# Products over the 16 meta tokens: reading 128 rows, 112 of them zero, in place of 16

## The reference

```python
u = rmsnorm(h, norm_g)                       # h: 16 meta tokens, then 512 tokens
hq, hf, hi, hz, aq, ak, av, az, ga, gb = split(u @ w_in)
# branch A, per head: gated linear recurrence, S_t = diag(f_t) S_{t-1} + k_t^T v_t, o_t = S_t^T q_t
f = lb + (1 - lb) * sigmoid(hf);  k = 1 - f;  v = hi
yA = (rmsnorm(oA, hg_norm_g) * silu(hz)) @ w_branch_a
# branch B, per head: differential attention in blocks of 128 queries, causal, meta keys always visible
p = softmax(q1 k1^T * scale) - lam * softmax(q2 k2^T * scale)
yB = (rmsnorm(p @ v, da_norm_g) * (1 - lam_init) * silu(az)) @ w_branch_b
m = sigmoid(ga) * yA + sigmoid(gb) * yB
out = rmsnorm(h + m @ w_out, final_g)[16:]   # the meta tokens are dropped
```

## Time and profile before

| | |
|---|---|
| median of 3 runs | 784.7 us (783.88 to 784.8) |
| profiled execution, span of the core | 782.7 us |
| mean granted TensorE clock | 0.995 of full speed |
| TensorE busy (matmul) | 762.8 us, 97% |
| TensorE weight load busy | 665.0 us, 85% |
| VectorE, ScalarE, GpSimd busy | 60%, 36%, 3% |
| DMA queue of the weights | 26.5% of 16 engines |

### The profile page before, as it was taken

The page is one execution under the profiler, slowest core; times in us unless marked ns, Lnnn a source line. Parts: engine busy times, 40 slices in busy tenths (PEclk is TensorE's granted clock), DMA queues, the critical chain, the costliest instruction groups (busy, mean ns, idle before and its releaser), DMA issues.

```text
span 782.7 us, 13096 instructions
## 1 busy us (share of the span) xinstructions
PE 762.8 (97%) x4689; PEld 665.0 (85%) x4689; DVE 468.4 (60%) x1085; ACT 282.2 (36%) x564; POOL 22.4 (3%) x30
## 2 busy tenths in 40 slices
PE   3999999999999999999999999999999999999996
PEld 2998899889889888988988998898888888888885
DVE  4667668658766865866785686587644333333342
ACT  5414432541452254144234415415532222222132
POOL 1000000000000000000000000000000000000001
PEclk9999999999999999999999999999999999999999
DMA  7411220230122023023112202301232332333602
GB/s 241 134 56 54 82 80 1 79 107 27 54 80 80 27 80 106 1 68 93 54 54 80 80 0 80 107 28 55 81 108 83 105 108 81 106 91 97 238 31 108
DMA packets 105416, 63.18 MB, mean 81 GB/s; under 512 B 2066, under 2 KB 100900, under 8 KB 105396
## 3 DMA queue, kind: packets, MB, share of 16 engines
q1 hardware_dynamic: 105076, 62.26, 26.5%
q10 hardware_dynamic: 320, 0.66, 0.3%
HBM read 60.81 MB, written 2.10 MB: 80 GB/s over the span
## 4 chain that ended last, share of the span: by engine, by line
PE 96%; SPq 1%; issue 1%; DMA 1%; DVE 0%; ACT 0%; POOLq 0%; POOL 0%; DVEq 0%; ACTq 0%
PE ps L361 26%; PE ps L362 25%; PE ps L363 25%; PE ps L469 3%; PE ps L544 3%; PE ps L573 2%; PE ps L574 2%; PE ps L453 1%; PE ps L564 1%; PE ps L551 1%; PE ps L510 1%; PE ps L509 1%; PE ps L476 1%; PE ps L516 1%; PE ps L492 1%
## 5 line engine op out<-in xcount | busy, mean ns | idle before, releaser
L361 PE MATMUL ps<-uT_hi,w_hi 128*128 128x264 f32 (+2 forms) x904 | 315.2, 349 | 0.0
L362 PE MATMUL ps<-uT_lo,w_hi 128*128 128x264 f32 (+2 forms) x904 | 299.0, 331 | 0.0
L363 PE MATMUL ps<-uT_hi,w_lo 128*128 128x264 f32 (+2 forms) x904 | 298.9, 331 | 0.0
L361 PEld LDWEIGHTS ps<-uT_hi,w_hi 128*128 128x128 f32 x904 | 171.2, 189 | 17.1
L363 PEld LDWEIGHTS ps<-uT_hi,w_lo 128*128 128x128 f32 x904 | 170.7, 189 | 16.2
L252 DVE TENSOR_TENSOR w_lo<-w_raw,w_hi 128x1024 fp32r<-128x1024 f32 x104 | 126.3, 1221 | 96.4 <-ACT w_hi L247 95.3
L362 PEld LDWEIGHTS ps<-uT_lo,w_hi 128*128 128x128 f32 x904 | 171.5, 190 | 12.5
L247 ACT ACTIVATE w_hi<-w_raw 128x1024 fp32r<-128x1024 f32 x104 | 110.0, 1057 | 87.8 <-PE ps L363 84.3
L778 ACT ACTIVATE e<-ps,small 128x144 f32<-128x144 f32 (+2 forms) x48 | 22.9, 483 | 71.5 <-DVE small L1179 71.5
L1125 DVE TENSOR_REDUCE small<-sq 128x4 f32<-128x512 f32 x16 | 11.0, 686 | 47.8 <-ACT sq L767 47.8
L1075 DVE TENSOR_TENSOR kk<-kk,tt 128x264 f32<-128x264 f32 (+1 forms) x48 | 20.6, 429 | 25.0 <-PE ps L469 20.7
(11 more groups left out here) (184 smaller groups left out, 1070.2 us busy)
## 6 DMA issues: line engine op xcount, KB each, us to landing
w_raw<-in_w_in SPq DMA_DIRECT2D x80, 512.0 KB, 3.7
w_raw<-in_w_branch_a SPq DMA_DIRECT2D x8, 512.0 KB, 3.6
w_raw<-in_w_branch_b SPq DMA_DIRECT2D x8, 512.0 KB, 3.6
w_raw<-in_w_out SPq DMA_DIRECT2D x8, 512.0 KB, 3.7
x_in<-in_x SPq DMA_DIRECT2D x4, 512.0 KB, 7.9
x_res<-in_x SPq DMA_DIRECT2D x4, 512.0 KB, 6.5
out<-y_out SPq DMA_DIRECT2D x8, 256.0 KB, 2.2
rope<-in_c_rope SPq DMA_DIRECT2D x1, 528.0 KB, 5.9
```

Source lines behind the costliest of these rows:

```text
L361: pe.matmul(dst, w[0], rhs[0], start=start, stop=False, skip_group_check=True)
L362: pe.matmul(dst, w[0], rhs[1], start=False, stop=False, skip_group_check=True)
L363: return pe.matmul(dst, w[1], rhs[0], start=False, stop=stop, skip_group_check=True)
```

## The change

Four fills ahead of the head loop set the meta tile of `pT`, `v_b`, `v_a` and `k_tok` to zero in all 128 rows. In the loop ScalarE and VectorE write rows 0 to 15 as before, and the two products read 128 rows. The fills add to `g_pre`, for which ScalarE waits ahead of the first head's sections, and VectorE in its preparation of the decay constants.

```diff
@@ block.gpsimd
             pool.memset(half_neg, -0.5).then_inc(g_pre, 1)
+            for tail in (pT[:, CH, :], v_b[:, CH, :], v_a[:, CH, :], k_tok[:, CH - 1, :]):
+                pool.memset(tail, 0.0).then_inc(g_pre, 1)
             pool.wait_ge(g_pre, 1)
@@ state_sums
-                pe.matmul(g[:, 0:P], k_tok[0:META, CH - 1, :], v_a[0:META, CH, :], start=True, stop=True) \
+                pe.matmul(g[:, 0:P], k_tok[:, CH - 1, :], v_a[:, CH, :], start=True, stop=True) \
                     .then_inc(hg_done, 1)
@@ attend
-                pe.matmul(dst, pT[0:META, CH, :], v_b[0:META, CH, :], start=False, stop=True) \
+                pe.matmul(dst, pT[:, CH, :], v_b[:, CH, :], start=False, stop=True) \
                     .then_inc(at_done, 1)
@@ block.scalar
+            act.wait_ge(g_pre, 5)
             for n in range(AHEAD):
@@ block.vector
+            dve.wait_ge(g_pre, 5)
             dve.wait_ge(a_pre, 3)
```

## The result

The changed kernel takes 770.02 us (median of 4 runs, 769.36 to 770.25) against 784.75 us (the kernel before, the three runs of above and one more): a ratio of 0.9817, 95% interval 0.9805 to 0.9829, which is 14.7 us off. The forecast was 770.6 us and 14.1 us off. The profiled execution has a span of 768.4 us, where the forecast said 768.6.

The account below looks back on a forecast made before the run. TensorE was taken as the bound, never waiting long in the head loop. Attention 12.5 us plus state sum 1.6 us made 14.1 us off: span 768.6 us, plus 2.0 us to the median, 770.6 us; full range 769.0 to 774.2.

Parts of the forecast that it names:

- The fills are hidden: Four GpSimd fills ahead of its first power: some 0.3 us each, 1.2 us in sum, wholly under 5.3 us idle.
- Rival 3: Fills at GpSimd's arithmetic rate, 77 us in all, hold up the start by 72 us: 842 us; chance 2%.
- The narrowest handover: VectorE's probabilities of block 2 to TensorE's transposes: 0.25 us of room left after the change, 0.06 us needed.
- rival 1: TensorE reaches block 2's transposes early and waits, giving back up to 0.40 us a head: 773.8 us; chance 12%.
- The weight slots have room of microseconds: Weight handovers to TensorE in the head loop: claimed microseconds of room, so no wait when TensorE gets there earlier.
- the two terms: Savings in the head loop: 12.5 us from 32 attention products and 1.6 us from 8 state-sum products.

Follow-up runs that it names:

- e1: Changed kernel with the state sum put back to 16 rows, so only the attention product reads 128 rows: 771.84 us, ratio 0.9838 to the kernel before.
- e6: Changed kernel with block 0's scores also reading 128 rows, using two zero-padded query copies per head on ScalarE: 770.46 us, ratio 0.9828 to the kernel before.
- e9: Changed kernel with only VectorE's copy for the low part of the next weight section moved ahead of level 6: 770.40 us, ratio 0.9820 to the kernel before.

## Why the prediction was right

- **TensorE is the bound and waits for nothing in the heads.** Right: its list of waits has the same three rows from the start of the kernel, and the saved time comes out of the head period one for one.
- **A change of height costs some 0.19 us, and the height itself nothing.** Right, and shown from four sides: the two parts alone (0.39 and 0.20 us a product), 96 rows (no cost), 64 rows (one change between sum and scores gone, none in attention), and another order in the sum (no change). For attention this is 4 x 8 x 0.39 = 12.5 us from the periods of e1, as forecast; for the state sum 1.6, as forecast. Blocks 0 and 1 both gave 0.39, where the prediction had 0.38 and 0.40. Its guess that the new weights are loaded with nothing beside them fits the rows of the loads; what goes on inside the engine no run shows. The Trainium skill's "TensorEngine Tiling (Array Packing)", section "Key Properties", says that changing the mode drains the engine. These runs agree in so far as each change of height costs 0.19 us and 96 rows beside 128 cost nothing; they don't show a drain as such. The Trainium skill's sentence that one matmul with K=32 takes as long as one with K=128 ("TensorE: Matmul & The Clock Gate", "Why this matters for your kernels") doesn't carry over to a short product in a stream of full ones: that product costs 0.39 us on top. No run here times one by itself.
- **The fills are hidden.** Right. GpSimd's timeline of the changed kernel:

```profile
0.78 0.20 POOL L343 MEMSET pT<- 128x128 f32 x1
...
1.20 0.20 POOL L343 MEMSET k_tok<- 128x128 f32 x1
6.10 0.55 POOL L349 TENSOR_TENSOR small<-small 128x1 f32<-128x1 f32 x1 [4.70 <-DVE small L956]
```

  0.20 us each (0.3 was estimated), all over by 1.4 us; the first power starts at 6.10 us. Rival 3 is out by 4.7 us of idle time.
- **The narrowest handover holds.** Right where it looked, 0.26 us of room for 0.25 forecast, and rival 1 did not come. The survey was incomplete, though. "The weight slots have room of microseconds" is wrong for the section behind level 7, whose low part is ready 0.05 us before its load, in the kernel before too (135.50 and 135.55 us). It cost the forecast nothing only because none of the saved changes lies between level 6, from which VectorE's chain starts, and this section. In e6 one did, and its saving was lost there.
- **The size.** 14.1 us forecast, 13.9 from the period, 14.7 by the medians. Each of the two terms is right where it is measured alone; with both in, a head saves 0.03 us less than their sum, 0.2 us in eight heads, and no run isolates why. What the 14.7 has above 13.9 is not in the heads of these traces; the stretch ahead of the first one and the spread of the runs are left for it. The changed kernel measured again is 784.25 - 770.49 = 13.8 us under the kernel before beside it.

## What to carry to other kernels

On a TensorE that never waits, count the places where the row height of neighbouring products changes, not the rows (16, 64, and 96 or 128 together, were three heights here). A lone short product between full ones got cheaper when its operands were filled up with zeros, once, ahead of the loop. For short products that already stand in pairs of one height it brought 0.05 us of 0.66 and took two copies a head (e6). Read the cost from the starts of neighbouring passes: the share of busy time says nothing (97% before and after), since the gap is inside what counts as busy. Before taking time out of one place, look for the next handover behind it that has no room, for each operand that TensorE waits for, the weights too.

## What the runs showed of the hardware

- Products of 64 rows, one on rows 0 to 63 and one on rows 64 to 127, start in pairs, 3 to 9 ns apart. They win back most of what their changes of height cost: two changes and two pairs took 0.66 us, four full-height passes 0.61 us, both with the section pass ahead.
- The stretch ahead of the first head differs from run to run by more than 1 us with the same instructions on TensorE: its first level product starts at 47.99 us before, 47.55 in the changed kernel, 48.46 in e9, 47.00 in the 64-row kernel, 46.71 in e6. The granted clock there differs as well, and doesn't explain it. The first 45 us of the kernel before and of the changed one (busy us and passes of each engine, then the granted clock):

```profile
0.00:45.00 45.00, 31.37 (x209) 29.88 (x210) 25.00 (x50) 20.54 (x34) 4.06 (x10) 0.92 0.58 182
```

```profile
0.00:45.00 45.00, 31.81 (x212) 30.11 (x213) 25.43 (x51) 20.57 (x35) 4.62 (x14) 1.00 0.59 185
```

  The changed kernel is three passes further on by then, at a mean clock of 1.00 for 0.92. The kernel before has 0.65 from 15 to 20 us and 0.67 from 20 to 25 us, behind a stretch in which TensorE waited for the normalised rows, so 1.2 GHz in a part of them and 2.4 GHz in the rest. It is tempting to put the 0.4 us ahead of the heads down to this, but the other traces don't bear it out. The changed kernel measured again has 0.62 from 15 to 20 us and 0.70 from 20 to 25 us and begins its first head only 0.18 us later (47.73). The 64-row kernel and e6 have 0.76 and 0.73 in the first of these stretches and begin sooner than any other; the 96-row kernel has 1.00 in both and begins at 47.93 us. What sets this stretch stays open.
